# Token loading, the first RMS norm, and the four layer norms of a two-block transformer kernel rearranged on one core

## What is computed

```python
h = concatenate([meta_tokens, x])                       # 16 + 256 rows
proj = rms_norm(h, norm_mix) @ w_in                     # the first norm
...                                                     # attention, RWKV-7, merge
h = h + (silu(gate_ffn) * up_ffn) @ w_ffn_out
h = rms_norm(h, norm_final)                             # end of the first block
h = layer_norm(h, ln_in_g, ln_in_b)                     # input norm, n = 0
for l in range(2):
    mix = attention(h @ w_in_2[l]) @ w_o_2[l]
    h = layer_norm(4 ** 0.25 * h + mix, ln1_g[l], ln1_b[l])            # n = 1, 3
    h = layer_norm(4 ** 0.25 * h + experts(h), ln2_g[l], ln2_b[l])     # n = 2, 4
return h
```

## Time and profile before

| | |
|---|---|
| median of 3 runs | 2400.44 us (2398.69 to 2403.57) |
| the profiled execution's own time | 2400.53 us |
| its span, first to last instruction | 2398.7 us |
| PE busy | 2347.3 us, 98% |
| PEld, DVE, ACT, POOL busy | 2095.4, 1684.5, 1301.3, 573.9 us |
| matmuls from the identity, L465 | dummies 16 + 100 + 2 x 40 + 50 and some smaller groups |

### The profile page before, as it was taken

The page is one execution under the profiler, slowest core; times in us unless marked ns, Lnnn a source line. Parts: engine busy times, 40 slices in busy tenths (PEclk is TensorE's granted clock), DMA queues, the critical chain, the costliest instruction groups (busy, mean ns, idle before and its releaser), DMA issues.

```text
span 2398.7 us, 42228 instructions
## 1 busy us (share of the span) xinstructions
PE 2347.3 (98%) x16485; PEld 2095.4 (87%) x16485; DVE 1684.5 (70%) x3068; ACT 1301.3 (54%) x2800; POOL 573.9 (24%) x440
## 2 busy tenths in 40 slices
PE   8999999999999999999999999999999999999998
PEld 7878989997899889999888887789989999888886
DVE  5745354446689778887776556869888888777556
ACT  6543345456564665545555555655665555555554
POOL 3626135555379000000000003378300000000000
PEclk9999999999999999999999999999999999999999
DMA  5311155554245556556776564245555656777554
GB/s 200 116 62 47 54 167 188 187 185 147 75 159 178 190 182 197 193 198 206 244 245 215 193 213 151 82 159 172 182 191 192 194 193 197 237 245 236 194 193 159
DMA packets 148150, 420.99 MB, mean 176 GB/s; under 512 B 15984, under 2 KB 49136, under 8 KB 147568
## 3 DMA queue, kind: packets, MB, share of 16 engines
q1 hardware_dynamic: 144080, 405.34, 51.9%
q0 software_dynamic: 2256, 8.99, 1.0%
q10 hardware_dynamic: 1616, 3.96, 0.4%
HBM read 400.40 MB, written 17.83 MB: 174 GB/s over the span
## 4 chain that ended last, share of the span: by engine, by line
PE 93%; DVE 3%; ACT 2%; POOL 1%; DMA 1%; issue 1%; ACTq 0%; DVEq 0%; SPq 0%
PE pb L465 92%; PE pb L474 1%; POOL lo L2635 1%; ACT arena L1334 1%; ACT hi L1322 0%; DVE arena L2284 0%; ACT arena L1528 0%; DMA cst<-in_consts 0%; DMA raw<-in_w_out 0%; DVE arena L1880 0%; DMA raw<-in_w_ffn_in 0%; DVE arena L1877 0%; DVE arena L2345 0%; ACT HT L1334 0%; ACT L1334 0%
## 5 line engine op out<-in xcount | busy, mean ns | idle before, releaser
L465 PE MATMUL pb<-HT,hi 128*128 128x256 f32 (+2 forms) x5232 | 1093.8, 302 | 3.9 <-POOL lo L2635 1.9
L1322 ACT CAST hi<-raw 128x512 fp32r<-128x512 f32 x1402 | 821.0, 620 | 372.8 <-PE pb L465 255.7
L465 PEld LDWEIGHTS pb<-HT,hi 128*128 128x128 f32 x5232 | 839.0, 191 | 42.6 <-issue 4.3
L465 PE MATMUL pb<-HT,lo 128*128 128x256 f32 (+1 forms) x2968 | 839.3, 283 | 0.0
L2635 POOL TENSOR_TENSOR lo<-raw,hi 128x512 fp32r<-128x512 f32 x384 | 525.3, 1390 | 437.1 <-ACT hi L1322 436.8
L1887 DVE TENSOR_TENSOR lo<-raw,hi 128x1024 fp32r<-128x1024 f32 x464 | 567.4, 1223 | 41.6 <-ACT hi L1322 41.4
L465 PEld LDWEIGHTS pb<-HT,lo 128*128 128x128 f32 x2968 | 566.6, 191 | 0.0
L465 PE MATMUL pb<-hi,WH 128*128 128x512 f32 x1112 | 433.2, 390 | 1.6 <-DVE WL L2569 1.1
L465 PE MATMUL pb<-lo,WH 128*128 128x512 f32 x1112 | 432.9, 389 | 0.0
L465 PE MATMUL pb<-hi,WL 128*128 128x512 f32 x1112 | 432.6, 389 | 0.0
L1334 ACT ACTIVATE arena<-pb 128x256 f32<-128x256 f32 (+2 forms) x216 | 82.4, 382 | 358.6 <-PE pb L465 355.6
(11 more groups left out here) (213 smaller groups left out, 2107.9 us busy)
## 6 DMA issues: line engine op xcount, KB each, us to landing
raw<-in_uT SPq DMA_DIRECT2D x256, 512.0 KB, 3.5
raw<-in_vT SPq DMA_DIRECT2D x256, 512.0 KB, 3.7
raw<-in_w_ffn_in SPq DMA_DIRECT2D x44, 512.0 KB, 3.8
raw<-in_wq SPq DMA_DIRECT2D x32, 512.0 KB, 3.5
wk<-kept SPq DMA_DIRECT2D x128, 128.0 KB, 3.5
raw<-in_w_in SPq DMA_DIRECT2D x24, 512.0 KB, 3.6
raw<-in_w_ffn_out SPq DMA_DIRECT2D x22, 512.0 KB, 4.4
raw<-in_w_gate SPq DMA_DIRECT2D x16, 512.0 KB, 3.2
```

Of the source, the lines that this page charges most:

```text
L465: return e.matmul(o, l, r, start=start, stop=stop)
L1322: e.copy(u.hi[k], u.half[k]).then_inc(*s.up("hi", ("hi", g)))
```

## The change

Line numbers in order rows are those of each file. It does the following.

1. `x1` goes on SP's queue ahead of the first weights; ACT's queue carries `x0`, `meta`, `ident`, `pk` in this order, with separate semaphores for the last two. POOL's four start-up loads wait for `x1`.
2. The squares: ACT squares `x0` only. DVE gets the mean squares of `meta` and then of `x1` with `BN_STATS`, `BN_AGGR` and mean squared plus variance.
3. The token tiles are no longer scaled. DVE scales the identity to a diagonal `DG` for each tile, and PE multiplies each token tile with it (a full fp32 matmul in place of a transpose). There are 18 dummies instead of 16.
4. `layer_norm` becomes three functions. `input_norm` (n = 0, 2) does what it did. `attention_norm` (n = 1, 3) runs block 0 to its root and first scaling before the last piece's statistics; block 1's half 0 is scaled on DVE, half 1 on ACT. `output_norm` (n = 4) folds mean and gain into one instruction, factor and bias into a second, all on DVE, with the root taken beside the first; POOL has no part.
5. Dummies: 100 become 44, 40 become 20 (twice), 50 become 24.
6. One unit of each layer, (0, 1) of `w_in_2`, gets both `lo` halves on POOL; before, DVE had one.

The core of the diff:

```diff
-                    low=both if (i, g) < (0, 2) else pool)
+                    low=both if (i, g) < (0, 1) else pool)
...
-    warm(7, 16)
+    warm(7, 18)
...
-            x = tp(PB[b][:, o:o + n], m.xs[0:n, i, c * 128:(c + 1) * 128])
+            x = mm(PB[b][:, o:o + n], m.tok[i][0][:, c * 128:(c + 1) * 128], m.DG[0:n, i * 128:i * 128 + n], True, True)
...
-    warm(2, 50)
-    warm(3, 50)
+    warm(2, 22)
+    warm(3, 22)
...
-        warm(2, 20)
-        warm(3, 20)
+        warm(2, 10)
+        warm(3, 10)
...
-            warm(2, 25)
-            warm(3, 25)
+            warm(2, 12)
+            warm(3, 12)
...
-    e.dma_start(m.Hv[:, 1, :], rows[:, 1, :]).then_inc(*s.up("x1_in", ("x", 1), by=16))
     e.dma_start(m.meta, m.d["meta_tokens"]).then_inc(*s.up("meta_in", ("meta",), by=16))
-    e.dma_start(m.pk[:, :], m.d["pack"]).then_inc(*s.up("pack_in", by=16))
-    e.dma_start(m.C("ident"), m.d["consts"][:, 0:128]).then_inc(*s.up("pack_in", ("ident",), by=16))
-    for j, i in enumerate((1, 2, 0)):
...
+    e.dma_start(m.C("ident"), m.d["consts"][:, 0:128]).then_inc(*s.up("ident_in", ("ident",), by=16))
+    e.dma_start(m.pk[:, :], m.d["pack"]).then_inc(*s.up("pack_in", ("pack",), by=16))
+    w.wait_ge(*s.to("x", 0))
+    fn(m.scr, m.Hv[:, 0, :], ACT.Square, acc=sm[:, 1:2]).then_inc(*s.up("squares", ("sq0",)))
...
+    for i, ready in ((0, ("meta",)), (2, ("x", 1))):
+        x, n = m.tok[i]
+        k, ms = i // 2, sm[0:n, 4 + i:5 + i]
+        w.wait_ge(*s.to(*ready))
+        for j in range(2):
+            e.bn_stats(m.ST6[0:n, k, j, :], x[:, j * 512:(j + 1) * 512]).then_inc(*up("norms"))
+        own()
+        e.bn_aggr(m.MV[0:n, k, :], m.ST6[0:n, k, :, :]).then_inc(*up("norms"))
+        own()
+        stt(ms, m.MV[0:n, k, 0:1], m.MV[0:n, k, 0:1], m.MV[0:n, k, 1:2], M, A).then_inc(*up("norms"))
+        own()
+        ts(ms, ms, 1.0, 1e-6, M, A).then_inc(*up("norms"))
...
     for i, (x, n) in enumerate(m.tok):
-        ts(m.xs[0:n, i, :], x, sm[0:n, 8 + i:9 + i], None, M).then_inc(*up("norms", *([("xs",)] if i == 2 else [])))
+        x = ts(m.DG[0:n, i * 128:i * 128 + n], C("ident")[0:n, 0:n], sm[0:n, 8 + i:9 + i], None, M)
+        x.then_inc(*up("norms", *([("diag",)] if i == 2 else [])))
...
+    def attention_norm(n, pieces, ready, src):
...
+        statistics(HALVES[:3], pieces, ready, src)
+        block_root(0)
+        block_inverse(0)
+        scaled(n, 0, 0, src(0, 0))
+        statistics([(1, 1)], pieces, ready, src)
+        block_root(1)
+        scaled(n, 0, 1, src(0, 1))
+        block_inverse(1)
+        shift(n)
+        scaled(n, 1, 0, src(1, 0))
+
+    def output_norm(pieces, ready, src):
+        statistics([(0, 0), (0, 1), (1, 0), (1, 1)], pieces, ready, src)
+        means(0, 1)
+        root_of(4)
+        w.wait_ge(*s.to("bc", 4))
+        for i, (t, k) in enumerate([(0, 0), (0, 1), (1, 0), (1, 1)]):
+            cs, bs = slice(k * 512, (k + 1) * 512), slice(1024 + k * 512, 1536 + k * 512)
+            stt(m.FP[:, t, cs], src(t, k), m.MV[:, t, 0:1], m.BC2[:, cs], S, M).then_inc(*up("last"))
+            if i == 0:
+                inverse(4)
+            own()
+            x = stt(m.Hv[:, t, cs], m.FP[:, t, cs], sm[:, 102 + t:103 + t], m.BC2[:, bs], M, A)
+            x.then_inc(*up("last", ("y_out", t, k)))
...
     d = m.d
+    w.wait_ge(*s.to("x", 1))
     e.dma_start(m.lora, d["lora"]).then_inc(*s.up("lora_in", by=16))
...
+    rows = m.d["x"].rearrange("b (t p) n -> p (b t) n", p=128)
+    e.dma_start(m.Hv[:, 1, :], rows[:, 1, :]).then_inc(*s.up("x1_in", ("x", 1), by=16))
     for i, u in enumerate(m.units):
```

More of the change, by code:

```diff
@@ L1302, in tensor @@
         emptied_by({(0, k): OUTV[0, k] for k in range(2)}, ("pre", l, 1))
-        for k in range(2):
-            free[OUTV[1, k]] = [("hn", 2 * l + 2, 1, k)]
         if l == 0:
-            warm(2, 25)
-            warm(3, 25)
+            for k in range(2):
+                free[OUTV[1, k]] = [("hn", 2, 1, k)]
+        if l == 0:
+            warm(2, 12)
+            warm(3, 12)
 def scalar(e, s, m):
@@ L1781, in scalar @@
         root_table()
-        norm_root(2 * l + 1, [m.XN[:, 1, 0:512], PB[OB[1, 1]][:, :]])
+        n = 2 * l + 1
+        for t in range(2):
+            w.wait_ge(*s.to("var_eps", n, t))
+            fn(sm[:, 102 + t:103 + t], sm[:, 100 + t:101 + t], ACT.Sqrt).then_inc(*s.up("roots", ("ln_root", n, t)))
+        w.wait_ge(*s.to("shift", n))
+        x = fn(m.Hv[:, 1, 512:1024], PB[OB[1, 1]][:, :], ACT.Identity, scale=sm[:, 103:104], bias=m.SHIFT)
+        x.then_inc(*s.up("norms_act", ("hn", n, 1, 1)))
         turned_biased(("exp", l), f"g1{l}", f"b1{l}", ("in", l), TURNS_EXP)
@@ L1852, in scalar @@
         root_table()
-        norm_root(2 * l + 2, [PB[OUTV[1, k]][:, :] for k in range(2)])
-    for t, k in HALVES:
+        if l == 0:
+            norm_root(2, [PB[OUTV[1, k]][:, :] for k in range(2)])
+    w.wait_ge(*s.to("var_eps", 4))
+    fn(sm[:, 102:104], sm[:, 100:102], ACT.Sqrt).then_inc(*s.up("roots", ("ln_root", 4)))
+    for t, k in ((0, 0), (0, 1), (1, 0), (1, 1)):
         cs = slice(k * 512, (k + 1) * 512)
@@ L2196, in vector, with statistics @@
             take("fout", j - 1)
-    def layer_norm(n, order, pieces, ready, src, extra=None):
+    def statistics(order, pieces, ready, src):
         def stats(t, k):
@@ L2207, in layer_norm, with means, root_of @@
                 stats(*order[i - 1])
-        stats(*order[3])
+        stats(*order[-1])
+    def means(*ts_):
         own()
-        for t in range(2):
+        for t in ts_:
             e.bn_aggr(m.MV[:, t, :], m.ST6[:, t, :, :]).then_inc(*up("stats"))
         own()
+    def root_of(n, extra=None):
         if extra is None:
@@ L2220, in layer_norm, with shift, scaled, input_norm @@
         own()
+    def shift(n):
         stt(m.SHIFT, m.MV[:, 1, 0:1], -1.0, sm[:, 103:104], M, M).then_inc(*up("stats", ("shift", n)))
-        for k in range(2):
-            cs = slice(k * 512, (k + 1) * 512)
-            x = ts(m.Hv[:, 0, cs], src(0, k), m.MV[:, 0, 0:1], sm[:, 102:103], S, M)
-            x.then_inc(*up("norms", ("hn", n, 0, k)))
+    def scaled(n, t, k, src):
+        cs = slice(k * 512, (k + 1) * 512)
+        x = ts(m.Hv[:, t, cs], src, m.MV[:, t, 0:1], sm[:, 102 + t:103 + t], S, M)
+        x.then_inc(*up("norms", ("hn", n, t, k)))
+    def input_norm(n, order, pieces, ready, src, extra=None):
+        statistics(order, pieces, ready, src)
+        means(0, 1)
+        root_of(n, extra)
+        inverse(n)
+        shift(n)
+        for k in range(2):
+            scaled(n, 0, k, src(0, k))
+    def attention_norm(n, pieces, ready, src):
+        def block_root(t):
+            means(t)
+            ts(sm[:, 100 + t:101 + t], m.MV[:, t, 1:2], 1e-5, None, A).then_inc(*up("stats", ("var_eps", n, t)))
+        def block_inverse(t):
+            w.wait_ge(*s.to("ln_root", n, t))
+            e.reciprocal(sm[:, 102 + t:103 + t], sm[:, 102 + t:103 + t]).then_inc(*up("stats"))
+            own()
[7 more added lines that the diff above has]
+        block_inverse(1)
+        shift(n)
+        scaled(n, 1, 0, src(1, 0))
+    def output_norm(pieces, ready, src):
+        statistics([(0, 0), (0, 1), (1, 0), (1, 1)], pieces, ready, src)
+        means(0, 1)
+        root_of(4)
[5 more added lines that the diff above has]
+                inverse(4)
+            own()
+            x = stt(m.Hv[:, t, cs], m.FP[:, t, cs], sm[:, 102 + t:103 + t], m.BC2[:, bs], M, A)
+            x.then_inc(*up("last", ("y_out", t, k)))
     def gain_step(i, tag, bc, n):
```

45 lines of the change are left out of this document (16 added, 29 removed).

## The result

The changed kernel takes 2394.27 us (median of 22 executions, 2387.54 to 2405.40), the kernel before 2400.47 on the same chip (22, 2398.69 to 2404.26). The ratio is 0.9972, 95% interval 0.9962 to 0.9983: faster by about 0.3%. The forecast was 2386.3 with a range of 2382.5 to 2391.5. Direction right, size less than half, and the time lies outside the range. The second thing to see is the spread: 5.6 us before, 17.9 us after. The profiled execution took 2395.41 us with a span of 2393.6, near the median.

What follows compares the result with a forecast made beforehand. PE was taken to bound the kernel, with 93% of the span on the last-ending chain. Savings of 2.0 + 5.7 + 2.3 + 2.4 + 1.8 = 14.2 from 2400.5 gave 2386.3 us, range 2382.5 to 2391.5.

Steps and rivals of the forecast that it cites:

- The start: Loads, statistics and token turns up to the first product: turns begin at 10.85, first product at 17.3, 2.0 us saved.
- A second record for each of two wide matmuls adds 0.2 a chunk: Token turns at the start: extra fp32 cost between 0 and 1.6 us in all, taken as 1.1.
- The clock rival: At the five dummy places: fewer dummies let TensorE's clock fall, 25.5 us lost in all, 2411.8 us; chance 0.04.
- late-tokens rival: Loads at the start: `meta` still lands at 9.4, the sum loses 3.6 us, 2389.9 us; chance 0.12.
- Four passes: Token turns: each fp32 turn costs four transposes' time, 17.9 us, first product at 28.8, 2397.8 us; chance 0.03.
- The weights: Behind input norm and layer 0: splits or loads not ready, gains return as waits for `lo`, 2394.4 us; chance 0.05.
- The input norm: End of the first block: fewer dummies and earlier DVE let PE turn at 543.85 instead of 549.58, 5.7 us saved.
- Behind layer 0: Norm after layer 0: DVE freed of a `lo` half, PE turns at 1469.5 instead of 1472.00, 2.4 us saved.
- The end: Output norm: all on DVE with POOL quiet, last gain done at 2394.5 instead of 2396.25, 1.8 us saved.
- The attention norms: The two norms after attention: PE turns at 658.45 instead of 659.61, 1.15 us saved each, 2.3 in all.
- one scaling 0.5: DVE comes to the last statistics at 656.0: Attention norm: block 0's small steps and first scaling delay DVE's last statistics by only 0.5 us.
- 0.3 to 1 us: In front of each turn: PE's expected idle time, used as the argument against a falling clock.

Runs made afterwards that it cites:

- e12: The changed kernel itself, unmodified, measured and profiled once more: 2396.23 us, ratio 0.9966 to the kernel before.
- e6: e4 with the old rule for `lo` halves put back (both engines make those of the second group of tiles too): 2395.88 us, ratio 0.9991.
- e1: The changed kernel with the start of the kernel before (points 1 to 3 undone), all norms as changed: 2391.65 us, ratio 0.9961.
- e7: e4 with the attention norms' scaling of half 0 of block 0 moved behind the last statistics: 2388.37 us, ratio 0.9934.
- e3: The changed kernel with 34 unused products ahead of the turns instead of 18: 2394.65 us, ratio 0.9969.
- e4: The changed kernel with tokens scaled on DVE and transposed instead of multiplied with a diagonal, and 26 unused products: 2390.97 us, ratio 0.9969.
- e10: The changed kernel with 26 unused products ahead of its fp32 turns instead of 18: 2393.25 us, ratio 0.9954.
- e5: The changed kernel with three unused products behind each of the eight chunks of fp32 turns: 2406.41 us, ratio 1.0010.

## Why the prediction was wrong

**The start: two steps failed, and one of them is the miss.** "A second record for each of two wide matmuls adds 0.2 a chunk" was mis-sized. At the full clock a chunk of fp32 turns takes 0.94 us (e12), against 0.67 a chunk in the kernel before from first turn to first product ((19.32 - 13.99) / 8): 0.27 more. The bound of 0.2 came from 128-wide matmuls back to back, and counted a second record for the two wide products alone; the narrow one has a second record too (the rows of two at 11.97 to 12.29 in e12). Here PE became the limit of the stage, where ACT and DVE had been, and all eight chunks count, 2.2 us where 1.1 were put in. The second step is one the text didn't have: it put the turns' cost at the full clock, while the unused products ahead of them were rows of 0.22, a clock not yet up. In the kernel before they run until 14.0, and the clock rose at 14.3 in the trace; the change begins the turns at 11.9, and at 1.2 GHz a chunk takes 1.65. The forecast moved the work forward and forgot that the clock's rise is on the same path. The clock rival put the risk at the norms and gave it 0.04; it belonged to the start, with a price of some 6 us in a third to a half of the executions.

By terms, with the clock up (e12): the turns begin at 11.97, not 10.85 (`meta` 6.85, not 5.8, which is a third of the late-tokens rival), 1.1 lost; turns 7.5 us, not 6.4, another 1.1. These 2.2 us are the 2.0 that should have been saved, and 0.2 more. Without the clock, 5.6 on top and 0.7 in the first product, which begins at 1.2 GHz (its third lo row: 1.12 us after its start before, 1.84 now).

**Four passes.** This rival gave 17.9 us of turns. The changed kernel took 13.2, which looks like halfway there, but at the low clock. At the full one an fp32 chunk takes 0.94 to 0.96 against 0.56 for a chunk of transposes, 1.7 times and not four. The rule of the Trainium skill ("FP8 and Floating Point Precision", TensorE Precision Notes), four passes for a true fp32 product, isn't what failed. In the trace of before the four records of the earlier trace rows start 0.11 us apart, as long as an unused product of 256 bf16 columns takes (11.09 / 100). So a record of 128 columns takes two passes' time, and two records take four, as the page has it. What failed is the step from four passes to four transposes: the transposes of a norm start 0.11 apart too, so each is worth two passes already.

**The weights** rival didn't come about: PE's one wait for `lo` behind the turns is 1.56 us at the input norm and 1.57 behind layer 0, before it was 1.56 at both.

**The input norm** was right: 5.65 of 5.7, turns at 550.34 minus marker 545.31 = 5.03, against 10.93 before. **Behind layer 0** was right, 2.28 of 2.4, and so was the reason (e6). **The end** was right, 1.65 of 1.8.

**The attention norms** gave 0.68 and 1.50 in this profile where 1.15 each were forecast. The sum looks right, the step doesn't: "one scaling 0.5: DVE comes to the last statistics at 656.0". It came at 657.85, because the scaling stood in GpSimd's way. In e1 both layers have the long form. The forecast had the rows of the same instruction at 0.99 for two, but these ran when POOL had nothing to do; that POOL would be in the midst of a subtraction at the new place wasn't looked up. It was worth 1.2 us a layer (e7). In the changed kernel's own profile it struck layer 0 alone, in e12 both layers.

**The clock behind the norms.** PE idled longer than the "0.3 to 1 us" of the forecast, and in e1, e3, e4 and e10 one stretch of 3.4 us at half clock stands behind the attention norm of layer 0, worth 1.3 to 1.5 us: between the markers the norm loses 0.6 us against before in e1 (from -5.12 to -4.53) and 0.7 to 0.9 in the three others, where with the same long scaling and no such stretch it gains 0.7 (changed kernel, e6, e12). In e5 one stands behind layer 1's norm, at 1600.9. The changed kernel's own two profiles don't show it there. The rival was right that it exists, and wrong in size: nowhere near 3.8 us a place.

**The range** went wrong because it took its edges from one profiled execution and 1.6 us of spread from before, where the three executions it names reach 3.1 above their median. Its upper edge also stopped at the late tokens, though the prediction's own lower bounds together save only 6.4, which is 2394.1; that this is nearly the time measured is luck, as it has the loss in other places. Nine of the 22 executions lie within the range, 2387.5 to 2391.1, and two just behind (2393.0, 2393.1). Six more are of the group with the slow start, and five have the long fall of the last section.

## What to carry to other kernels

Work that is moved ahead of the clock's rise is to be priced at 1.2 GHz, with its own rows at that clock, and the end of the unused products is part of the critical path at the start. Look at what the turn costs at the low clock, not only at the full one: transposes lose 0.1 us a chunk there, fp32 products 0.7. Whenever a scaling from SBUF to SBUF is moved on VectorE, look up what GpSimd does at its new place. And where a row of unused products is cut, the engine that they cover for must be shown to be earlier, by its own row.
